# Fifty-four products of a tile of ones at the start of TensorE's program, ahead of the first real multiplication

## The reference, cut to what matters

```python
def rmsnorm(x, g):
    xf = x.astype(jnp.float32)
    y = xf * lax.rsqrt(jnp.mean(xf * xf, axis=-1, keepdims=True) + EPS)
    return (y * g.astype(jnp.float32)).astype(x.dtype)
...
def rglru_mixer(h, w_in, conv_w, conv_b, w_ra, b_ra, w_ix, b_ix, lam, w_out):
    B, S, _ = h.shape
    u = h @ w_in
    xb, yb = u[..., :D_RNN], u[..., D_RNN:]
...
def first_block(...):
    h = x
    for layer in range(DEPTH):
        hn = rmsnorm(h, norm_g[layer, 0])
        if layer < N_A_LAYERS:
            h = h + rglru_mixer(hn, ...)
```

## Time and profile before

| | |
|---|---|
| Median of 3 runs | 1723.3 us (1723.25 to 1723.79) |
| Span of the profiled execution, which is the time that the profile gives for it | 1723.1 us |
| TensorE busy | 1699.8 us, 99% of the span |
| VectorE, ScalarE, GpSimd busy | 1265.2, 833.4, 375.8 us |
| First matmul starts | 10.42 us after the span's start |
| Time that TensorE waited, by the view of waits | 10.4 us before its first matmul, ten reasons in all |

### The profile page before, as it was taken

How to read it: one execution, slowest core, us unless ns; L and a number is a source line. 1 busy time by engine, 2 the same in 40 slices (tenths; PEclk the granted TensorE clock), 3 DMA queues, 4 the chain that set the end, 5 groups by cost and what they waited for, 6 DMA issues and landing times.

```text
span 1723.1 us, 31820 instructions
## 1 busy us (share of the span) xinstructions
PE 1699.8 (99%) x12958; PEld 1596.8 (93%) x12958; DVE 1265.2 (73%) x1657; ACT 833.4 (48%) x1104; POOL 375.8 (22%) x425
## 2 busy tenths in 40 slices
PE   7999999999899999999999999999999999999999
PEld 7799999898789998999989999998999989999997
DVE  7898889786868889798757876666666665676663
ACT  5875444444655444444453255444444435554442
POOL 0222012535404223600032140002100128330000
PEclk9999999999999999999999999999999999999999
DMA  8246567685106777565646445464445544335560
GB/s 318 106 150 210 197 221 256 228 303 181 58 13 221 249 272 263 180 203 178 229 154 232 150 148 192 173 225 164 167 175 210 205 155 160 124 134 193 194 228 33
DMA packets 50711, 321.02 MB, mean 186 GB/s; under 512 B 7696, under 2 KB 8912, under 8 KB 20144
## 3 DMA queue, kind: packets, MB, share of 16 engines
q1 hardware_dynamic: 36432, 280.61, 46.0%
q0 software_dynamic: 12736, 36.87, 6.6%
q10 hardware_dynamic: 1440, 2.10, 0.3%
HBM read 307.39 MB, written 10.09 MB: 184 GB/s over the span
## 4 chain that ended last, share of the span: by engine, by line
PE 96%; DVE 2%; ACT 1%; issue 1%; DMA 0%; ACTq 0%
PE bank L2285 19%; PE bank L2286 19%; PE bank L2287 19%; PE bank L2291 18%; PE bank L2292 9%; PE bank L2464 1%; PE bank L2572 1%; PE bank L2939 1%; PE bank L2891 1%; PE bank L2646 1%; PE bank L2757 1%; PE bank L2582 1%; PE bank L2533 1%; PE bank L2534 1%; PE bank L2535 1%; PE bank L2477 1%
## 5 line engine op out<-in xcount | busy, mean ns | idle before, releaser
L1459 DVE TENSOR_TENSOR w_lo<-raw,w_hi 128x1024 fp32r<-128x1024 f32 (+2 forms) x486 | 643.6, 1327 | 270.6 <-ACT w_hi L1029 269.3
L1029 ACT ACTIVATE w_hi<-raw 128x1024 fp32r<-128x1024 f32 (+2 forms) x486 | 538.3, 1115 | 576.2 <-PE bank L2287 346.1
L2285 PE MATMUL bank<-hg_hi,w_hi 128*128 128x256 f32 x2648 | 754.3, 285 | 11.3 <-DVE hg_lo L1464 10.4
L2286 PE MATMUL bank<-hg_lo,w_hi 128*128 128x256 f32 x2648 | 750.3, 283 | 0.0
L2287 PE MATMUL bank<-hg_hi,w_lo 128*128 128x256 f32 x2648 | 750.2, 283 | 0.0
L2285 PEld LDWEIGHTS bank<-hg_hi,w_hi 128*128 128x128 f32 x2648 | 509.0, 192 | 16.0 <-DVE w_lo L1459 10.8
L2286 PEld LDWEIGHTS bank<-hg_lo,w_hi 128*128 128x128 f32 x2648 | 509.2, 192 | 0.2
L2287 PEld LDWEIGHTS bank<-hg_hi,w_lo 128*128 128x128 f32 x2648 | 509.2, 192 | 0.0
L2291 PE MATMUL bank<-hid,w_hi 128*128 128x512 f32 x1056 | 372.9, 397 | 0.0
L2292 PE MATMUL bank<-hid,w_lo 128*128 128x256 f32 x1056 | 296.3, 281 | 0.0
L2291 PEld LDWEIGHTS bank<-hid,w_hi 128*128 128x128 f32 x1056 | 198.5, 188 | 48.2 <-issue 1.0
(11 more groups left out here) (412 smaller groups left out, 1909.0 us busy)
## 6 DMA issues: line engine op xcount, KB each, us to landing
raw<-in_w SPq DMA_DIRECT2D x189, 1024.0 KB, 4.9
raw<-in_w SPq DMA_DIRECT2D x48, 1408.0 KB, 6.4
raw<-in_w SPq DMA_DIRECT2D x8, 768.0 KB, 5.4
b_rows<-in_s_b_rows POOLq DMA_DIRECT2D x8, 512.0 KB, 7.6
l_rows<-s_powers POOLq DMA_DIRECT2D x64, 64.0 KB, 8.5
s_ca<-cp_s POOLq DMA_DIRECT2D x8, 512.0 KB, 4.5
s_ba<-ba_s POOLq DMA_DIRECT2D x8, 512.0 KB, 7.4
ba_slot<-s_ba POOLq DMA_DIRECT2D x8, 512.0 KB, 5.2
```

Of the source, the lines that this page charges most:

```text
L1029: act.activation(w_hi[s][:, 0:n], raw[r][:, c * n:(c + 1) * n], ACT.Copy).then_inc(hi_made, 1)
L1459: dve.tensor_tensor(w_lo[s][:, 0:n], raw[r][:, c * n:(c + 1) * n], w_hi[s][:, 0:n].bitcast(F32), ALU.subtract).then_inc(lo_made, 1)
L2285: pe.matmul(psum, w_hi_ap, x_hi_ap, start=first, stop=False, **kw)
L2286: pe.matmul(psum, w_hi_ap, x_lo_ap, start=False, stop=False, **kw)
```

## The change: products of ones ahead of the phases

TensorE's program gets a new start. It waits until `ones_d` is filled (`pool_const` at 1), multiplies `ones_d` with itself 40 times into columns 0 to 127 of bank 7, waits until the first half of the weights has its `w_hi` (`hi_made` at 1), and does 14 more. Nothing reads these results. Then the phases follow as they were.

```diff
@@ -46,6 +46,7 @@
 RT = 12
 GT = 3
+BUSY_BEFORE = (40, 14)
@@ -3011,6 +3012,16 @@
+            def keep_busy(products):
+
+                for _ in range(products):
+                    pe.matmul(bank[7][:, 0:P], ones_d[:, :], ones_d[:, :], start=True, stop=True)
+
+            pe.wait_ge(pool_const, 1)
+            keep_busy(BUSY_BEFORE[0])
+            pe.wait_ge(hi_made, 1)
+            keep_busy(BUSY_BEFORE[1])
             for ph in phases:
                 if ph["kind"] == "ffn":
                     ffn_phase(ph)
```

## The result

The changed kernel takes 1728.65 us (median of 8 executions, 1726.71 to 1732.14); the kernel before beside it 1723.28 us (8 executions, 1722.96 to 1727.03). The medians lie 5.4 us apart. The ratio on record, which is not that of the two medians, is 1.0024, with a 95% interval of 1.0013 to 1.0035: 4.1 us slower (2.2 to 6.0). The forecast was 1726.0 with a range up to 1727.3, so the direction of the sum was right and the time lies above the range.

What follows compares the result with a forecast made beforehand. TensorE, busy 99% of the span, was taken to bound the kernel. 5.5 - 2.4 - 0.4 = +2.7 us on the 1723.1 span gives 1725.8, plus 0.2 for the median: 1726.0, range 1722.6 to 1727.3.

Steps and rivals of the forecast that it cites:

- What bounds the kernel: TensorE's list runs nearly without a gap behind its first matmul, so a delay at its start moves the end as much.
- The price of a product: Each product of ones at TensorE's start is two records: 0.218 us at the upper clock, 0.43 at the lower.
- The start: First product of ones on TensorE at 1.1 us, just after the tile of ones is filled.
- the rise: TensorE's clock goes from 1.2 to 2.4 GHz 6.11 us after it begins work, at 7.2 us.
- half 0: First real matmuls begin at 15.9 instead of 10.42 us (+5.5), but run at the upper clock (-2.4).
- The sum, +2.7: Net delay from TensorE's start: 5.5 later, less 2.4 on the first real matmuls and 0.4 on L2310.
- The row on L2836: Same-shape products, 16 in 3.49 us, 0.218 each; by it the work to release the clock outlasts the wait it fills.
- The 1720.5: Time by the skill's keep-busy rule alone: the slow stretch at the start vanishes, 2.4 + 0.4 us saved.
- the lost fall: Rival: the clock drop at 446.60 us does not happen, up to 3.4 us back, about 1722.6; chance 0.06.
- That the products fit into the wait: Rival: one record a product, so first real matmuls still begin at 10.42 at full clock; -2.4 us, 1720.9; chance 0.08.
- That the clock does not rise: Rival: products of ones leave TensorE at the lower clock; +13.9 us, 1737.2; chance 0.05.
- An early rise: Rival: upper clock granted well before 6.11 us of work at TensorE's start, 1723.0 to 1724.5; chance 0.07.

Runs made afterwards that it cites:

- short kernel: Sparse attention layer left out: kernel before 1531.82 us, changed kernel 1534.59 (+2.77), with 22 and 6 products 1530.29 (-1.53).
- the idle waits: No products, TensorE waits idle for the third rest of weights (1730.51 us, ratio 1.0032) or first squares (1727.49, ratio 1.0019), against the kernel before.

## Why the prediction was wrong

**What bounds the kernel** was read rightly as far as 340 us: TensorE's list has no gap there but one of 0.2 us, the first stretch is at the lower clock, and a delay at the start passes whole to the end of the short kernel.

**The price of a product** (two records, 0.218 fast, 0.43 slow) measured 0.223 and some 0.43. **The start** (1.1) was 1.01, **the rise** (7.2) about 7.0, **half 0** (15.9) 15.93, the second wait held nothing, and half 0 ran at steps of 0.12. **The sum, +2.7**, measured +2.78 in the profiled pair and +2.77 in the short kernels. That the rise came at 7.0 was luck: in the other three profiles of the changed kernel the fast steps begin between 5.4 and 5.7 us. It did no harm to the sum, because in the kernel before the rise moves as well (TensorE runs slow for 6.1, 4.6 and 4.3 us in its three profiles) and half 1 follows by half as much in both: 21.43 to 22.15 changed, 18.44 to 19.37 before, means 2.9 apart. The prediction let the rise vary in the changed kernel only. The row on L2836, by which the products are longer than the wait that they fill, was right.

The Trainium skill ("TensorE: Matmul & The Clock Gate", "Why this matters for your kernels") asks for TensorE to be kept busy without a break. The 1720.5 that this alone would have given did not come with 54 products; with 28, which fit into the wait, its gain was there at half 1 (17.12, 2.25 us earlier than in the earlier trace rows), though not in the whole kernel's time (1723.58, ratio 0.9998); without the attention phase 22 and 6 products gained 1.5 us.

**The step that failed** is the one that turned the sum into a time: "the median of the runs shown is 0.2 above that span, so 1726.0". It takes the three runs shown, 1723.3, for what this kernel takes, and it lays a span beside times that include 1.9 us around theirs. With the 1.9 the profiled execution stands at about 1725.0, more than any of the three runs shown, and that would have warned that executions of this kernel differ by more than the 0.5 us of these three. On the median of all its executions, 1724.6, the same sum gives 1727.3 to 1727.4, at the edge of the range: this step is 1.3 of the 2.65 us by which the forecast was short. The eight executions of the kernel before beside the result include these three and are low too, 1723.28; its sets here have medians from there to 1726.10.

**The other half of the miss** is a term that the sum put at nothing: what the attention phase makes of the change. The whole kernel shows 4.3 us where the start gives 2.8; the 1.5 between them is the remainder above, and its cause stays open. "There is no later wait for the memory" was read from one execution in which VectorE's wait for `vc_other` did not show. In the short kernels no later wait swallowed the delay, as the prediction said; with the attention phase in the kernel the change costs that 1.5 us more.

**The range** failed with both. Its ends were the lost fall below and the bounds of the clock's rise above; the spread of the attention phase, 7.7 us from the lowest to the highest execution of the kernel before, was not a term.

**The rivals.** That the products fit into the wait: wrong for the change; a kernel with one record a product did not fit either, as its clock did not rise. That the clock does not rise: wrong for these products, right for that other kernel. An early rise: the profiled executions show half 1 between 21.43 and 22.15, so it does vary, by 0.7, and as much without the change. That the fall is lost: it was, in the first profiled execution of four, and it gave back 1.3 to 1.5 us, not 3.4, since TensorE then waited for `prob`.

## What to carry to other kernels

Products that are to keep an engine busy cost their own time as soon as they outlast the wait: price them by records at the clock of that stretch, and count how many fit between the first moment that they can run and the first real input. Before a small effect is put to a time, find out by how much one execution differs from the next, and compare spans with spans; and where one phase makes that spread, take the phase out of both kernels and measure the effect in what is left.

## What the runs showed of the hardware that was not expected

Products of a tile of ones raised TensorE's clock or did not. Plain fp32 products at 0.21 a record had the upper level at about 7.0 in the first profile of the changed kernel, 6 us after they began, and 3.0 to 6.0 us after it in all eleven profiled executions that have them. The fp32r products, at the same 0.21 a record and without a gap from 1.15 to 12.73, had not got it in 11.6 us; it came near the end of half 0, under the real matmuls. This was seen in one profiled execution, and what in the products makes the difference is not shown: half 0's matmuls read fp32r tiles too, and after the idle waits, with no product before them, their steps became fast within 3.6 and 4.6 us.

The upper level was lost within an idle time of 3.40 us (14 products; granted 0.50 from 9.80 to 13.10, though TensorE was busy again from 10.32). The place of the fall in the attention phase moved between executions of one kernel: 446.60 in the earlier trace rows, 434.9 or earlier in the second and third profile of the kernel before; no fall in the changed kernel's first profile, and one at 449.2 to 449.5 in its other three.
